# Memory keys and values computed at the start of the program, beside the first modulation tiles, and kept in DRAM

## The reference, cut to what matters

```
mod   = silu(c) @ w_ada + b_ada           # modulation, 6 parts of 2048; shift and scale first
mod_c = silu(c_ctx) @ w_ada + b_ada
hc = rmsnorm(ctx, norm1_w) * (1 + csc1) + csh1     # into the state-space branch (xbc tiles)
hl = rmsnorm(x, norm1_w) * (1 + sc1) + sh1
...                                       # mixer, MLP, then the second block
x = x + merged @ w_out                    # out2
hc   = rms_norm(x, g_cross)
memn = rms_norm(mem, g_mem)
q = hc @ w_q;  k, v = split(memn @ w_kv)  # q: 16 tiles, kv: 32 tiles
x = x + softmax(q k^T / sqrt(512)) v @ w_o
```

## Time and profile before

| | |
|---|---|
| median of three runs | 4567.77 us |
| the profiled execution: its own time | 4558.99 us |
| its span (first to last instruction) | 4557.2 us |
| granted TensorE clock, mean | 0.974 |
| PE / POOL / DVE / ACT busy, share of span | 95% / 76% / 53% / 39% |
| read from DRAM over the span | 800.06 MB, 176 GB/s |

### The profile page before, as it was taken

The page is one execution under the profiler, slowest core; times in us unless marked ns, Lnnn a source line. Parts: engine busy times, 40 slices in busy tenths (PEclk is TensorE's granted clock), DMA queues, the critical chain, the costliest instruction groups (busy, mean ns, idle before and its releaser), DMA issues.

```text
span 4557.2 us, 66685 instructions
## 1 busy us (share of the span) xinstructions
PE 4330.2 (95%) x24622; PEld 3670.3 (81%) x24622; DVE 2413.0 (53%) x3748; ACT 1754.7 (39%) x1996; POOL 3481.0 (76%) x2520
## 2 busy tenths in 40 slices
PE   8899989899999999999988998999999999999997
PEld 1577755788888888888877886899888888888886
DVE  3326775333332365533254312698867847875784
ACT  1234422344444453434434432443333333333333
POOL 0357750788888887978977984898888898898886
PEclk9999979999999999999999999999999999999999
DMA  8356750445555444445544552444454454454443
GB/s 312 131 192 267 294 207 3 181 169 186 191 184 184 179 173 162 177 161 188 187 148 157 185 190 90 170 169 167 176 184 169 173 185 175 166 185 176 176 174 122
DMA packets 111127, 805.21 MB, mean 177 GB/s; under 512 B 12903, under 2 KB 13192, under 8 KB 14088
## 3 DMA queue, kind: packets, MB, share of 16 engines
q1 hardware_dynamic: 108720, 787.30, 48.0%
q10 hardware_dynamic: 2200, 14.90, 0.9%
HBM read 800.06 MB, written 2.10 MB: 176 GB/s over the span
## 4 chain that ended last, share of the span: by engine, by line
PE 56%; POOL 18%; DVE 8%; issue 6%; ACT 1%; POOLq 0%; DMA 0%; DVEq 0%; ACTq 0%
PE psum L513 30%; POOL w_lo L437 18%; PE psum L517 15%; PE psum L643 2%; DVE hid L2861 1%; PE psum L502 1%; PE psum L504 1%; PE psum L503 1%; DVE out_hl L2865 1%; DVE out_hl L2863 1%; PE psum L1205 1%; PE psum L796 1%; PE psum L784 1%; PE psum L1159 0%; DVE mix_m L2108 0%
## 5 line engine op out<-in xcount | busy, mean ns | idle before, releaser
L437 POOL TENSOR_TENSOR w_lo<-ring,w_hi 128x512 fp32r<-128x512 f32 x2416 | 3111.3, 1313 | 784.6 <-ACT w_hi L1281 782.4
L1281 ACT ACTIVATE w_hi<-ring 128x1024 fp32r<-128x1024 f32 x1232 | 1296.9, 1060 | 1886.8 <-PE psum L517 1625.9
L513 PE MATMUL psum<-hc_hl,w_hi 128*128 128x512 f32 x5120 | 1310.7, 398 | 42.3 <-DVE hc_hl L1844 13.1
L513 PEld LDWEIGHTS psum<-hc_hl,w_hi 128*128 128x128 f32 x5120 | 925.1, 190 | 222.1 <-issue 31.0
L517 PEld LDWEIGHTS psum<-hc_hl,w_lo 128*128 128x128 f32 x5120 | 700.8, 191 | 53.2 <-POOL w_lo L437 2.1
L517 PE MATMUL psum<-hc_hl,w_lo 128*128 128x256 f32 x5120 | 715.8, 283 | 1.1 <-POOL w_lo L437 1.1
L513 PE MATMUL psum<-out_hl,w_hi 128*128 128x512 f32 x2048 | 520.0, 396 | 20.9 <-DVE x L2875 18.2
L513 PEld LDWEIGHTS psum<-out_hl,w_hi 128*128 128x128 f32 x2048 | 372.6, 191 | 89.3 <-DVE x L2875 18.9
L466 POOL TENSOR_TENSOR ada_acc<-ada_acc,ada_row 128x2048 f32<-128x2048 f32 x56 | 255.6, 4565 | 63.7 <-ACT ada_row L1393 59.2
L517 PEld LDWEIGHTS psum<-out_hl,w_lo 128*128 128x128 f32 x2048 | 281.5, 192 | 20.3
L517 PE MATMUL psum<-out_hl,w_lo 128*128 128x256 f32 x2048 | 287.3, 283 | 0.0
(11 more groups left out here) (452 smaller groups left out, 5354.0 us busy)
## 6 DMA issues: line engine op xcount, KB each, us to landing
ring<-stream SPq DMA_DIRECT2D x652, 1024.0 KB, 4.8
ring<-mixed SPq DMA_DIRECT2D x96, 1024.0 KB, 7.0
x<-x ACTq DMA_DIRECT2D x2, 2048.0 KB, 11.3
ctx_raw<-ctx ACTq DMA_DIRECT2D x1, 2048.0 KB, 9.6
mem_raw<-mem ACTq DMA_DIRECT2D x1, 2048.0 KB, 9.2
out<-x SPq DMA_DIRECT2D x4, 512.0 KB, 2.6
filt_w<-filt_w ACTq DMA_DIRECT2D x1, 1024.0 KB, 11.2
dft<-dft ACTq DMA_DIRECT2D x1, 1024.0 KB, 13.0
```

Of the source, the lines that this page charges most:

```text
L437: m = pool.tensor_tensor(w_lo[:, slot, c:c + 4], ring[:, s, h * KC // 2 + c:h * KC // 2 + c + 4], w_hi[:, slot, c:c + 4].bitcast(F32), ALU ...
L513: pe.matmul(psum[:, b, :].rearrange("p (s t) -> p s t", s=2), w_hi[:, slot, c], x_hl[c], start=start(c), stop=False, skip_group_check=True)
L1281: act.activation(w_hi[:, 2 * (s % 2) + h], ring[:, s, k], ACT.Copy).then_inc(hi_ready, 1)
```

## The change

The stream now begins with the 32 `kv` tiles, which are split as all others; `ada` leaves the stream. Its 32 tiles are cut anew (half as many output columns and twice as many inputs: 512 columns by four groups of 128 inputs, four tiles for one sum) and come in a ring of their own (`ada_in`), loaded behind `kv` tile n as the table ADA_AT says: one each for n below 28, two at n = 6, 13, 20, 27. Even ones are multiplied by PE as before. Odd ones are summed by DVE: eight operations of 128x512 each (4 input groups, 2 conditions), `ada_in` times a per-partition scalar plus an accumulator in PSUM, the last pair into SBUF; PE then sums over partitions with 32 matmuls of one column (`ada_turn`, side 1), beside 16 transposes for the even ones.

`kv` results go through `kv_out` (three buffers) to a DRAM tensor `kv_dram`, 128 KB a tile, issued by ACT (`keys_store`), and come back in two loads of 2 MB on ACT's queue, in `gate` and at the start of `out2`. `q` follows `out2` at once: ACT scales x for it while `out2` runs, DVE makes the low parts after tiles 6, 10, 14 and at the end, and `out2` reads `c_hl` in place of `h_hl`, since `q` needs the latter. The sum of the cross norm is on PE after q's tile 3.

```diff
-STREAM = [("ada", ADA_1), ("xbc", XBC), ("out1", KC), ("mlp", 2 * MLP_H),
+STREAM = [("kv", 2 * KC), ("xbc", XBC), ("out1", KC), ("mlp", 2 * MLP_H),
...
-          ("out2", KC), ("kv", 2 * KC), ("q", KC), ("o", KC), ("pq", KC), ("peer", 2 * EXPERT_B)]
+          ("out2", KC), ("q", KC), ("o", KC), ("pq", KC), ("peer", 2 * EXPERT_B)]
...
@@ sync
+        for n in range(2 * KC):
+            if n >= RING:
+                sp.wait_ge(lo_ready, 2 * n - 6)
+            load(n, n % RING)
...
+            for m in ADA_AT[n]:
+                if m >= 4:
+                    sp.wait_ge(ada_dve if m % 2 else ada_pe, (m - 4) // 2 + 1)
+                sp.dma_start(ada_in[:, m % 4], a["ada"][m].rearrange("p (k n) -> p k n", n=512)).then_inc(mix_landed[m % 4], 16)
@@ tensor
+        for n in range(2 * KC):
+            tile("kv", n, mem_hl[:], "mem")
+            for at_, side, g in TURN_AT:
+                if at_ == n:
+                    ada_turn(side, g)
+            for m in ADA_AT[n]:
+                if m % 2 == 0:
+                    ada_rows_pe(m // 2)
+            if n == 1:
+                norm_pe("mem", column=True)
...
         for n in range(KC):
-            tile("out2", n, h_hl)
-            if n == 12:
-                norm_pe("mem", column=True)
+            tile("out2", n, c_hl)
         for n in range(KC):
-            tile("kv", n, mem_hl[:], "mem")
-            if n == 13:
+            tile("q", n, h_hl, "cross")
+            if n == 3:
                 norm_pe("cross", row=False, column=True)
@@ scalar
+        for n in range(2, 2 * KC + 2):
+            split_tile(n, n // RING, n % RING)
...
+            if 3 <= n:
+                keys_store(n - 3)
...
+            if n in (30, 31, 32, 33):
+                scaled_high(n - 30)
@@ vector
+            for k in range(4):
+                for v in range(2):
+                    c, acc = 4 * (u % 4) + k, psum[:, 5 + v, :]
+                    src, scalar = ada_in[:, m % 4, k], c_silu[:, 4 * (u % 4) + k, v:v + 1]
...
+                        i = dve.scalar_tensor_tensor(ada_sums_[:, g % 2, v] if c == KC - 1 else acc, src, scalar, acc,
+                                                     ALU.mult, ALU.add)
...
+        for n in range(29):
+            for m in ADA_AT[n]:
+                if m % 2 and m > 3:
+                    ada_sums_dve(m // 2)
+            for g in range(4):
+                if PE_AT[4 * g + 3] + 1 == n:
+                    ada_rows_out(g)
+            keys_out(n)
...
+            if q == 2:
+                dve.wait_ge(half_done, 2 * FIRST["xbc"])
```

More of the change, by code:

```diff
@@ L92 @@
 RING = 4
-SPLIT0 = FIRST["xbc"]
+SPLIT0 = 0
+ADA_AT, _m = [], 0
+for _n in range(2 * KC):
+    _c = 0 if _n >= 28 else 2 if _n % 7 == 6 else 1
+    ADA_AT.append(list(range(_m, _m + _c)))
+    _m += _c
+PE_AT = {m // 2: n for n in range(2 * KC) for m in ADA_AT[n] if m % 2 == 0}
+DVE_AT = {m // 2: n for n in range(2 * KC) for m in ADA_AT[n] if m % 2 == 1}
+TURN_AT = sorted([(PE_AT[4 * g + 3] + 1, 0, g) for g in range(4)] + [(DVE_AT[4 * g + 3] + 1, 1, g) for g in range(4)])
+TURNED = {(side, g): i + 1 for i, (n, side, g) in enumerate(TURN_AT)}
+MOD_0 = 320
 NATIVE = ZB + HYENA
@@ L159, in build @@
     norm_part = at("norm_part", [P, 2, T], 200)
-    mod_rows = at("mod_rows", [2, ADA_1 * P], 88)
+    ada_in = at("ada_in", [P, 4, 4, 512], 88)
+    ada_sums_ = at("ada_sums", [P, 2, 2, 512], 128)
+    mod_rows = at("mod_rows", [2, 2, 512], 136)
+    kv_out = at("kv_out", [P, 3, T], 203)
     ada_acc = at("ada_acc", [P, 2, D], 40)
@@ new lines, in ada_turn @@
+        def ada_turn(side, g):
+            for j in range(4):
+                n0 = MOD_0 + 2 * (4 * (2 * g + side) + j)
+                if side == 0:
+                    if j == 0:
+                        pe.wait_ge(ada_copied, g + 1)
+                    i = pe.transpose(psum[:, 7, n0:n0 + 2], mod_rows[:, g % 2, j * P:j * P + P], const[0:2, IDENT, 0:2])
+                else:
+                    if j == 0:
+                        pe.wait_ge(ada_dve, 4 * g + 4)
+                    for v in range(2):
+                        i = pe.matmul(psum[:, 7, n0 + v:n0 + v + 1], ada_sums_[:, g % 2, v, j * P:j * P + P],
+                                      const[:, ONES, 0:1], start=True, stop=True)
+            i.then_inc(ada_turned, 1)
@@ L589, in _ @@
-        for n in range(ADA_1):
-            m = pe.transpose(psum[:, 6, 2 * n:2 * n + 2], mod_rows[:, n * P:n * P + P], const[0:2, IDENT, 0:2])
-        m.then_inc(ada_turned, 1)
         def dt_products():
@@ L1653, in _ @@
                 act.wait_ge(d_lo, DIL_HG)
-                act.dma_start(mem_raw[:], a["mem"]).then_inc(norm_in, 16)
+                for s in range(3):
+                    act.wait_ge(kv_stored[s], 16 * len(range(s, 2 * KC, 3)))
+                act.dma_start(kv[:, KC:], kv_dram[:, KC:]).then_inc(kv_back, 16)
             if n >= DIL_TILES:
@@ new lines, in _ @@
+        for q in range(4):
+            dve.wait_ge(norm_hi, q + 1)
+            for k in range(4 * q, 4 * q + 4):
+                m = dve.scalar_tensor_tensor(mem_lo[:, k], mem_raw[:, k], col("mem", k), mem_hi[:, k].bitcast(F32),
+                                             ALU.mult, ALU.subtract)
+            m.then_inc(norm_lo, 1)
+        norm_half_sum("mem", 0)
+        norm_half_sum("mem", 1)
+        ada_sums_dve(0)
+        dve.wait_ge(norm_sum, NH["mem"] + 1)
+        st.did(dve.tensor_scalar(nrt[:], psum[:, 7, 0:T], 1.0 / D, EPS, ALU.mult, ALU.add))
@@ new lines, in _ @@
+        st.settle()
+        dve.tensor_scalar(r_col[:, MEM], psum[:, 7, T:T + 2], 1.0 / D, EPS, ALU.mult, ALU.add).then_inc(norm_ms, 1)
+        ada_sums_dve(1)
+        dve.wait_ge(norm_rt, NI["mem"] + 1)
+        st.did(dve.reciprocal(r_row[:], nrt[:]))
+        st.did(dve.reciprocal(r_col[:, MEM], r_col[:, MEM]))
+        st.settle()
+        for n in range(29):
[6 more added lines that the diff above has]
+            keys_out(n)
+            if n == 9:
@@ L3049, in layout @@
     arrays = dict(
-        consts, stream=stream, mixed=mixed, cols=cols, c=c, x=acts(one["x"]), ctx=acts(one["ctx"]), mem=acts(one["mem_2"]),
+        consts, stream=stream, mixed=mixed, ada=ada_rows(one["w_ada"][:, :ADA_1 * P]), cols=cols, c=c, x=acts(one["x"]), ctx=acts(one["ctx"]), mem=acts(one["mem_2"]),
         wdt=dt_.reshape(KC, P, 32).transpose(1, 0, 2),
```

314 lines of the change are left out of this document (182 added, 132 removed).

## The result

The changed kernel takes 4506.89 us, the median of four runs (4505.12 to 4515.38), beside 4564.68 us for four runs of the kernel before (4560.6 to 4571.03). The ratio is 0.9876 with a 95% interval of 0.9857 to 0.9894, and the difference of the medians is 57.8 us. The forecast was 57.2 us less, 4510.5 us, with 4486 to 4538 as its range. The direction and the size came out as forecast. What is left to find out is whether the reasons did too, since a sum of ten terms can be right by errors that cancel.

A forecast was written before the change was run, and what follows sets the result against it. PE's own queue, busy 95% of the span, was taken as the bound. Front 138.8 + 3.0 behind out2 + 1.0 column sums - 200.0 removed = -57.2 us, so 4567.8 becomes 4510.5 us, range 4486 to 4538.

The forecast's parts named there:

- The start, 18.8 us: Front: c_silu near 13.3 us, then scaling and low parts of mem about 5.5 us more before PE's first product.
- the waits until tile 4 ends, 10.6 us: Front: PE waits as the inputs come in four pieces, ready near 18.8, 25, 29.5 and 31.2 us.
- 32 tiles and 64 matmuls: Front: PE takes 178.8 us for 32 kv tiles and 57.4 us for 16 modulation tiles.
- Small products, 9.0 us: Front, on PE: memory norm 2.0, two others 1.03 each, 16 transposes 1.1, 32 one-column products 4 x 0.95 us.
- POOL held up by the scalings, 4.2 us: Front: two scalings of 128x4096 delay POOL beyond its spare time, 2.1 us each.
- The passage, 12.8 us: Passage to xbc: PE waits 5.6 us for tile 0's split, 5.3 for round four, loses about 2 more.
- DVE's sums, 0.75 us: Front: each 512-column sum with SBUF and PSUM inputs takes 0.75 us, 96 us for 16 tiles; PE stays the bound.
- rival 3: Front: DVE's sums wait for POOL at 1.78 us each, 69 us more, 4580 us; chance 0.03.
- Removed, 200.0: Keys stage 189.6 us; in out2 a wait of 6.66, slow clock 1.75 and the memory's norm 2.0 us go.
- added behind out2, 4.0: After out2: 3.0 us for q's wait and slower clock, 1.0 us for the cross norm's column sums.
- the first: Front slots: in-order hand-offs cost 1 us in each of 28 slots, 28 us back, 4540 us; chance 0.16.
- The second: Till tile 27's end: DMA sets the pace, 12 us if queues give only 290 GB/s, 4523 us; chance 0.06.

The follow-up runs named there:

- all_pe: Changed kernel with all 32 modulation tiles multiplied by PE and none summed by DVE: 4554.19 us, ratio 0.9979 to the kernel before.
- late_split: Changed kernel with POOL's and ACT's split of xbc's tile 1 moved behind the fourth round of scaling: 4498.85 us.
- dve_half: Changed kernel with 48 more DVE sums (36 us of work) in 12 of DVE's modulation tiles: 4508.19 us, ratio 0.9859.
- before_again: Kernel before, unchanged, profiled a second time: this execution took 4576.65 us.
- again: Changed kernel, unchanged, measured and profiled a second time: 4504.0 us, ratio 0.9868.
- dma_more: Changed kernel with 16 more loads of 1 MB in the keys stage, into a place nothing reads: 4506.12 us, ratio 0.9871.
- sbuf_acc: Changed kernel with DVE's accumulators of the modulation sums in SBUF instead of two PSUM banks: 4531.36 us.

## Why the prediction was right, step by step

- **The start, 18.8 us, and the waits until tile 4 ends, 10.6 us.** Measured: 19.52, and tile 4's end at 64.93 where 66 was forecast. The four pieces came near 19.5, 25.1, 29.8 and 31.3 (forecast 18.8, 25, 29.5, 31.2). DVE's low parts, line 2068, took 472 ns at least and 1506 at most, as in the earlier trace rows.
- **32 tiles and 64 matmuls.** Right: a modulation tile on PE takes 3.60 us, and after the first products of the memory PE does not wait once for any engine until xbc.
- **Small products, 9.0 us: a term mis-sized.** I gave 32 one-column products 4 x 0.95 us, from a row that says x8. Those eight records are four matmuls, and one group has 4 x 2 = 8. A group takes 1.95 us, with its transposes 2.36, so the term is 4.5 us larger: 4 x (2.36 - 0.95) less the 1.1 of the transposes, which had their own.
- **POOL held up by the scalings, 4.2 us: not there.** The scalings took 5.02 and 5.57 us, and beside the second one POOL took 7.60 us for three low parts instead of 3.9. POOL did lose those microseconds, and PE had none of them: it was not close enough to POOL.
- **A slow clock, not in the sum.** Without any wait the clock fell for a while near 205 and 263 us (windows at 0.93): a modulation tile of 5.29 us instead of 3.60, a row of keys products of 3.24 instead of 2.00. From tile 5 to the end of the keys PE takes 213.5 us, where 27 x 5.59 + 13 x 3.59 + 4 x 2.36 + 2 x 1.03 = 209.1: about 4.4 us. Both times a group of one-column products stands directly before. `all_pe`, which has no such group, keeps the full clock (1.00 from 60 to 330 us). The three, +4.5, -4.2 and +4.4, and -1.1 from the start make 3.6 us; between the end of the keys as forecast (278.8) and as measured (281.9) lie 3.1. So the front's sum is right in part by luck: the scalings' term and a passage forecast 2.5 us too long paid for what was left out.
- **The passage, 12.8 us.** Measured 303.13 - 281.9 - 10.9 = 10.3. The wait of 5.6 us for xbc's split was not there, as DVE had two rounds done before PE came; the wait for round four was (5.86 for a forecast of 5.3), preceded by 1.46 for round three and followed by slow matmuls of 0.63 instead of 0.39 us. `late_split` shows POOL as the cause.
- **DVE's sums, 0.75 us.** Measured 0.747. `dve_half` shows that they had some 36 us of room, and `all_pe` that the matmuls they replace are worth 50 us. DVE's other work, as listed in the forecast, adds up to 56 us and not to some 61; with PE the bound nothing in the forecast hangs on it, and in rival 3 it moves 69 us to 64.
- **Removed, 200.0, and added behind out2, 4.0.** Forecast 196.0 for the stretch, measured 196.3. The query product's first tile waits 2.32 us, within its bounds; out2 has no wait for the memory's norm.
- **Not forecast: the 8.6 us in the middle,** which are a difference between executions and weigh little in a median.
- **Not forecast: 4.5 us in the attention over the memory.** Its first product to the first of the output product takes 61.1 us before and 56.6 now, and this does last: 61.2 in `before_again`, 56.7 in `again`, and in all ten profiles with the new order, `all_pe` among them, the first three of the four rows of `v_mem` run at full clock. The waits inside are the same; the same matmuls ran at the higher clock. Before, the last three of four rows of 16 records took 6.71, 5.11 and 5.76 us, and now 3.72, 3.72 and 5.65. The first two of these before, then the three now:

```profile
2764.93 6.71 PE L1159 MATMUL psum<-mem_pt,v_mem 128*128 128x256 f32 x16 [0.78 <-DVE mem_pt L2711]
...
2778.41 5.11 PE L1159 MATMUL psum<-mem_pt,v_mem 128*128 128x256 f32 x16 [0.79 <-DVE mem_pt L2711]
```

```profile
2716.63 3.72 PE L1200 MATMUL psum<-mem_pt,v_mem 128*128 128x256 f32 x16 [0.79 <-DVE mem_pt L2863]
...
2727.11 3.72 PE L1200 MATMUL psum<-mem_pt,v_mem 128*128 128x256 f32 x16 [0.78 <-DVE mem_pt L2863]
...
2738.06 5.65 PE L1200 MATMUL psum<-mem_pt,v_mem 128*128 128x256 f32 x16 [0.78 <-DVE mem_pt L2863]
```

The code there is unchanged; what stands ahead of it is not, since the loads of `kv` and the query product come in another order. No run takes that apart, so the cause stays open. The medians of the two measurements say 57.8 and 59.3 us against a forecast of 57.2, and with the 4.5 us left out they would say 53 to 55: still within the range, but the closeness to 57.2 is luck to that extent.

Of the rivals, the first had a chance of 0.16 and shows no trace: no idle time stands before the w_lo products. The second is refuted by `dma_more`. The third is refuted for this kernel by the row of 747 ns, and `sbuf_acc` shows the mechanism at work when the second input is in SBUF, though it then bites much earlier than the sum of totals had said. The Trainium skill, page SBUF — State Buffer, section Who interferes with whom, names two inputs in SBUF or a two-port mode as the condition. The first half agrees (0.75 us alone, up to 1.79 beside POOL). For the second half, the scaling of one SBUF input that `late_split` freed went from 5.23 to 1.38 us for four; no run here shows its mode.

## What to carry to other kernels

A product of a narrow vector with a wide matrix costs PE a full pass for almost no result: here it paid to sum half of it on DVE beside PE's real work. One of DVE's two inputs should lie in PSUM: with both in SBUF 27 of the 59 us were lost. How far that goes is not a matter of totals: 36 us more on DVE cost nothing and 67 us cost 27, and the wait came at a hand-off whose place in PE's queue was fixed right behind the sums, so look at who must follow the longest block of the helper. And before you explain a difference of a few microseconds in a stage that the change doesn't touch, profile the kernel before a second time.
